# Handing part of a mixer's tail from VectorE and ScalarE to GpSimd, with two engines' work in another order

## What is computed

```python
def second_block(x, c, ...):
    h = _rms(x, norm1_w) * (1 + sc1) + sh1
    u, q, k, v = jnp.split(h @ w_in, ...)
    y_ssm  = _s5(u, ...)                       # 512 wide, 32 groups of 64 complex states
    y_attn = _swa_sink(_rms(q), _rms(k), v, rel_bias, sinks)   # 8 query heads, 2 kv heads, window 128
    mixed = concat(_rms(y_ssm, out_norm_ssm), _rms(y_attn, out_norm_attn))
    x = x + g1 * (mixed @ w_out)
    x = x + g2 * _conv_ffn(_rms(x, norm2_w) * (1 + sc2) + sh2, ...)

def _s5(u, ...):
    s = associative_scan(a * s + b u)          # complex states: s_re, s_im
    z = gelu(s_re @ c_re - s_im @ c_im + d * u)
    return z * sigmoid(z @ w_glu + b_glu)
```

## Time and profile before

| | us |
|---|---|
| median of 3 runs | 1794.73 |
| lowest to highest | 1794.62 to 1794.98 |
| the profiled execution | 1793.39 |
| its span, first to last instruction | 1791.9 |

### The profile page before, as it was taken

The page is one execution under the profiler, slowest core; times in us unless marked ns, Lnnn a source line. Parts: engine busy times, 40 slices in busy tenths (PEclk is TensorE's granted clock), DMA queues, the critical chain, the costliest instruction groups (busy, mean ns, idle before and its releaser), DMA issues. The chain is left out here.

```text
span 1791.9 us, 23429 instructions
## 1 busy us (share of the span) xinstructions
PE 1763.9 (98%) x8822; PEld 1437.1 (80%) x8822; DVE 1069.7 (60%) x1507; ACT 729.3 (41%) x1001; POOL 186.1 (10%) x239
## 2 busy tenths in 40 slices
PE   9999999999999999999999999999999999999998
PEld 6888888888887777788877888887986788888887
DVE  7666546655655676656888743436595655566433
ACT  4222222333435877423333222225465355555322
POOL 4222001210000000005211110210000300000000
PEclk9999999999999999999999999999999999999999
DMA  7777423343222121224554552325122222222232
GB/s 246 238 221 221 134 74 96 98 138 99 90 95 94 48 66 53 71 94 150 173 188 125 158 158 66 107 93 187 68 79 68 93 95 94 94 94 82 94 95 81
DMA packets 171694, 206.81 MB, mean 115 GB/s; under 512 B 18404, under 2 KB 150114, under 8 KB 171106
## 3 DMA queue, kind: packets, MB, share of 16 engines
q1 hardware_dynamic: 144994, 161.97, 27.9%
q0 software_dynamic: 12640, 38.55, 6.7%
q10 hardware_dynamic: 13984, 5.27, 1.1%
HBM read 190.29 MB, written 17.56 MB: 116 GB/s over the span
## 5 line engine op out<-in xcount | busy, mean ns | idle before, releaser
L692 ACT CAST w_hi<-w_raw 128x2048 fp32r<-128x2048 f32 x158 | 301.8, 1911 | 722.4 <-PE bank L2004 360.9
L1188 DVE TENSOR_TENSOR w_lo<-w_raw,w_hi 128x2048 fp32r<-128x2048 f32 x158 | 367.3, 2325 | 358.4 <-ACT w_hi L692 357.7
L2004 PE MATMUL bank<-h_hi,w_hi 128*128 128x512 f32 x1056 | 412.3, 390 | 3.5 <-DVE w_lo L1188 2.2
L2004 PE MATMUL bank<-h_hi,w_lo 128*128 128x512 f32 x1056 | 411.1, 389 | 0.0
L2004 PE MATMUL bank<-h_lo,w_hi 128*128 128x512 f32 x1056 | 325.4, 389 | 1.6 <-DVE h_lo L1231 1.6
L2004 PEld LDWEIGHTS bank<-h_hi,w_hi 128*128 128x128 f32 x1056 | 198.2, 188 | 49.5 <-issue 3.4
L2004 PEld LDWEIGHTS bank<-h_lo,w_hi 128*128 128x128 f32 x1056 | 198.2, 188 | 43.3 <-DVE h_lo L1231 2.0
L2004 PEld LDWEIGHTS bank<-h_hi,w_lo 128*128 128x128 f32 x1056 | 198.3, 188 | 41.0
L1961 PE MATMUL bank<-hid_hi,w_hi 128*128 128x512 f32 x528 | 205.6, 389 | 0.0
L1961 PE MATMUL bank<-hid_hi,w_lo 128*128 128x512 f32 x528 | 205.4, 389 | 0.0
L1961 PE MATMUL bank<-hid_lo,w_hi 128*128 128x512 f32 x528 | 205.4, 389 | 0.0
(11 more groups left out here) (442 smaller groups left out, 2464.8 us busy)
## 6 DMA issues: line engine op xcount, KB each, us to landing
w_raw<-in_w_in SPq DMA_DIRECT2D x29, 1024.0 KB, 5.0
mod_raw<-in_w_mod POOLq DMA_DIRECT2D x96, 256.0 KB, 4.1
w_raw<-in_ffn_w_gate SPq DMA_DIRECT2D x22, 1024.0 KB, 5.2
w_raw<-in_ffn_w_up SPq DMA_DIRECT2D x22, 1024.0 KB, 5.2
w_raw<-in_w_up SPq DMA_DIRECT2D x22, 1024.0 KB, 4.9
w_raw<-in_ffn_w_down SPq DMA_DIRECT2D x16, 768.0 KB, 4.6
w_raw<-in_ffn_w_down SPq DMA_DIRECT2D x16, 640.0 KB, 4.0
w_raw<-in_w_out SPq DMA_DIRECT2D x8, 1024.0 KB, 5.0
```

The costliest lines, as they stand in the source:

```text
L692: act.copy(w_hi[i % 2][:], w_raw[i % 2][:]).then_inc(S("w_hi_done"), 1)
L1188: dve.tensor_tensor(w_lo[s][:], w_raw[s][:], w_hi[s][:].bitcast(F32), ALU.subtract).then_inc(S("w_split"), 1)
L2004: mm = pe.matmul(bank[:], w[:, k, at], h[:, k, :], start=k == first and part == 0 and i == 0, stop=k == last and part == 1)
```

## The change

- POOL computes the second part (imaginary) of the states in both halves: two products with `rotc` into `tmp[:, 4:6]` and one sum of 504 columns. DVE keeps the first part, and waits ahead of the second half's products until both parts of the first half are made, since POOL reads the scans' results.
- POOL computes the low parts of two panels, `PART["glu"][0]` between the two halves of the states, and the next one after the squares of `yat`.
- POOL squares `yat` for query blocks 0 to 2 and adds the four tiles, so that one tile of 384 columns is left to TensorE's sum; ACT squares the last block alone, in one instruction. POOL squares the first three tiles of `ys` and adds them; ACT squares the fourth. TensorE sums five products (384 and 4 x 128 columns) for `pa` and two for `ps`, instead of four and four of 512.
- DVE takes the last unit's two copies to `pT` and the last two copies to `yat` (`sw_last`), between the first two and the last two tiles of `z_lo`.
- ACT runs `sw_exp(7)` ahead of `chunk_out(3)`; TensorE runs `within_chunks(3)` after `turn_back(1)` and `sw_turn(6)` ahead of `turn_back(3)`.

```diff
@@ pool
+            def split(n):
+                pool.wait_ge(S("w_hi_done"), n + 1)
+                pool.wait_ge(S("w_split"), n)
+                pool.tensor_tensor(w_lo[n % 2][:], w_raw[n % 2][:], w_hi[n % 2][:].bitcast(F32), ALU.subtract).then_inc(S("w_split"), 1)
+            def second_part(half):
+                own = slice(NS // 2 * half, NS // 2 * half + NS // 2)
+                parts = [tmp[:, 4 + i, :].rearrange("p (s c) -> p s c", c=NC) for i in range(2)]
+                pool.wait_ge(S("scanned"), NS * (half + 1))
+                for i in range(2):
+                    done(pool.tensor_tensor(parts[i], scan_t[:, 2 * i + 1], rotc[:, 1 - i, own], ALU.mult))
+                pool.tensor_tensor(state[:, 1, own, 1:NC], parts[0][:, :, 0:NC - 1], parts[1][:, :, 0:NC - 1], ALU.add).then_inc(S("scan_out"), 1)
+            second_part(0)
+            split(PART["glu"][0])
+            second_part(1)
+            pool.wait_ge(S("sw_s"), 2 * len(SW_UNITS))
+            for b in (0, 2):
+                at = slice(b * P, min(b + 2, 3) * P)
+                pool.wait_ge(S("sw_out"), 2 * min(b + 2, 3))
+                done(pool.tensor_tensor(yat_sq[:, :, at], yat[:, :, at], yat[:, :, at], ALU.mult))
+                done(pool.tensor_tensor(yat_sq[:, 0:2, at], yat_sq[:, 0:2, at], yat_sq[:, 2:4, at], ALU.add))
+                ins = pool.tensor_tensor(yat_sq[:, 0, at], yat_sq[:, 0, at], yat_sq[:, 1, at], ALU.add)
...
+            ins.then_inc(S("yat_squared"), 1)
+            split(PART["glu"][0] + 1)
+            for t in range(3):
+                pool.wait_ge(S("glu_out"), t + 1)
+                done(pool.tensor_tensor(ys_sq[:, t, :], ys[:, t, :], ys[:, t, :], ALU.mult))
+                if t:
+                    ins = pool.tensor_tensor(ys_sq[:, 0, :], ys_sq[:, 0, :], ys_sq[:, t, :], ALU.add)
...
+            ins.then_inc(S("ys_squared"), 1)
             norm("p2", "mix2")
@@ act
             chunk_out(2)
+            sw_exp(7)
             chunk_out(3)
-            sw_exp(7)
             sw_turned(6)
             s5_gelu((2,))
-            sw_turned(7)
             s5_gelu((3,))
-            sw_out(6)
-            sw_out(7)
             act.wait_ge(S("sw_out"), len(SW_UNITS))
-            for k in range(4):
-                act.activation(yat_sq[:, k, :], yat[:, k, :], ACT.Square).then_inc(S("yat_squared"), 1)
+            act.activation(yat_sq[:, :, 3 * P:], yat[:, :, 3 * P:], ACT.Square).then_inc(S("yat_squared"), 1)
...
-            for k in range(4):
-                act.wait_ge(S("glu_out"), k + 1)
-                act.activation(ys_sq[:, k, :], ys[:, k, :], ACT.Square).then_inc(S("ys_squared"), 1)
+            act.wait_ge(S("glu_out"), 4)
+            act.activation(ys_sq[:, 3, :], ys[:, 3, :], ACT.Square).then_inc(S("ys_squared"), 1)
@@ dve, chunks
+                if half:
+                    dve.wait_ge(S("scan_out"), 2)
...
-                for part, (first, second, op) in enumerate(((cosine, sine, ALU.subtract), (sine, cosine, ALU.add))):
-                    done(dve.tensor_tensor(t[0], t[1], first, ALU.mult))
-                    done(dve.tensor_tensor(t[2], t[3], second, ALU.mult))
-                    ins = dve.tensor_tensor(state[:, part, own, 1:NC], t[0][:, :, 0:NC - 1], t[2][:, :, 0:NC - 1], op)
...
+                done(dve.tensor_tensor(t[0], t[1], cosine, ALU.mult))
+                done(dve.tensor_tensor(t[2], t[3], sine, ALU.mult))
+                dve.tensor_tensor(state[:, 0, own, 1:NC], t[0][:, :, 0:NC - 1], t[2][:, :, 0:NC - 1], ALU.subtract).then_inc(S("scan_out"), 1)
@@ dve
+            def sw_last():
+                dve.wait_ge(S("sw_t_out"), SW_BEFORE[7])
+                dve.wait_ge(S("sw_pv"), 6)
+                for kb in SW_BLOCKS[7]:
+                    dve.wait_ge(S("sw_t"), SW_BEFORE[7] + kb + 1)
+                    dve.tensor_copy(pT[:, 1, kb, :], B[2 + kb][:]).then_inc(S("sw_t_out"), 1)
+                for u in (6, 7):
+                    b, n = SW_UNITS[u]
+                    dve.wait_ge(S("sw_pv"), u + 1)
+                    dve.tensor_copy(yat[:, 2 * n:2 * n + 2, b * P:(b + 1) * P], B[7][:, 0:2 * P].rearrange("p (j q) -> p j q", j=2)).then_inc(S("sw_out"), 1)
...
             sw_scale(6)
-            split(PART["glu"][0])
             sw_scale(7)
-            z_split(range(4))
-            split(PART["glu"][0] + 1)
+            z_split((0, 1))
+            sw_last()
+            z_split((2, 3))
@@ pe, norm
+                if name in ("pa", "ps"):
+                    bank = sum_bank(name)
+                    if name == "pa":
+                        pe.wait_ge(S("yat_squared"), 2)
+                        pe.matmul(bank[:, 0:3 * P], ones[:], yat_sq[:, 0, 0:3 * P], start=True, stop=True)
+                        mm = products(bank[:, 3 * P:], [(ones[:], yat_sq[:, k, 3 * P:]) for k in range(4)])
+                    else:
+                        pe.wait_ge(S("ys_squared"), 2)
+                        mm = products(bank[:], [(ones[:], ys_sq[:, t, :]) for t in (0, 3)])
+                    mm.then_inc(S("norm_summed"), 4)
+                    return
@@ pe
             within_chunks(2)
-            within_chunks(3)
             turn_back(0)
             sw_scores(6)
             sw_scores(7)
             sw_values(4)
             turn_back(1)
+            within_chunks(3)
             sw_values(5)
             from_states(2)
             from_states(3)
             turn_back(2)
+            sw_turn(6)
             turn_back(3)
-            sw_turn(6)
             sw_turn(7)
```

More of the change, by code:

```diff
@@ L673, in _ @@
             pool.dma_start(bias[:], bass.AP(band_dram, P - 1, [[BAND - 1, P], [P * BAND, NQ], [1, 2 * P]])).then_inc(S("bias_landed"), 16)
+            def split(n):
[19 more added lines that the diff above has]
+                ins = pool.tensor_tensor(yat_sq[:, 0, at], yat_sq[:, 0, at], yat_sq[:, 1, at], ALU.add)
+                if b == 0:
+                    done(ins)
+            ins.then_inc(S("yat_squared"), 1)
[5 more added lines that the diff above has]
+                    ins = pool.tensor_tensor(ys_sq[:, 0, :], ys_sq[:, 0, :], ys_sq[:, t, :], ALU.add)
+                    if t == 1:
+                        done(ins)
+            ins.then_inc(S("ys_squared"), 1)
             norm("p2", "mix2")
@@ L1796, in chunks @@
                 dve.wait_ge(S("scanned"), NS * (half + 1))
-                for part, (first, second, op) in enumerate(((cosine, sine, ALU.subtract), (sine, cosine, ALU.add))):
-                    done(dve.tensor_tensor(t[0], t[1], first, ALU.mult))
-                    done(dve.tensor_tensor(t[2], t[3], second, ALU.mult))
-                    ins = dve.tensor_tensor(state[:, part, own, 1:NC], t[0][:, :, 0:NC - 1], t[2][:, :, 0:NC - 1], op)
-                    ins.then_inc(S("scan_out"), 1)
-                    dve.wait_ge(S("scan_out"), 2 * half + part + 1)
+                done(dve.tensor_tensor(t[0], t[1], cosine, ALU.mult))
+                done(dve.tensor_tensor(t[2], t[3], sine, ALU.mult))
+                dve.tensor_tensor(state[:, 0, own, 1:NC], t[0][:, :, 0:NC - 1], t[2][:, :, 0:NC - 1], ALU.subtract).then_inc(S("scan_out"), 1)
             n = PART["q2"][0]
@@ L1973, in norm @@
                         square = tmp[:, d % 6, :]
[L1974 to L1979, removed]
                     else:
```

## The result

| | before | after |
|---|---|---|
| median, us | 1794.69 (9 runs, 1791.55 to 1796.57) | 1799.72 (9 runs, 1799.3 to 1805.05) |
| span of the profiled execution, us | 1791.9 | 1798.3 |
| VectorE busy, us | 1069.7 | 1080.0 |
| POOL busy, us | 186.1 | 217.9 |
| TensorE busy, us | 1763.9 | 1763.0 |

The changed kernel is slower: ratio 1.0034, 95% interval 1.0026 to 1.0043, so 4.7 to 7.7 us. The forecast was 1802.7 us in a range of 1793.5 to 1806.0. VectorE gave work away and is busy 10.3 us longer: the first sign that it stood still inside its instructions.

What follows compares the result with a forecast made beforehand. TensorE, busy 98% of the span, was taken as the bound. 9.2 - 1.93 + 1.9 - 1.72 + 0.1 = +7.5 us, with +0.5 for the clock +8.0, gave 1802.7 us; range 1793.5 to 1806.0.

Steps and rivals of the forecast that it cites:

- the clock: TensorE's turns, values and `glu(0)` after idling: between -1.6 us and +2 us, taken as +0.5 us.
- second rival: Tail: collisions spare the two probability multiplications, 1794.3 us; or long POOL instructions admit VectorE four times, 1799.4 us; chance 0.19.
- deciding step: Tail: VectorE and POOL, both reading SBUF, wait for each other's whole instruction; price its remainder less 0.14 us.
- first rival: Tail: VectorE runs free beside POOL, `glu(0)` 2.0 us earlier, sums give 3.65: -5.6, so 1789.1 us; chance 0.19.
- Step 1: States' first half: VectorE's and POOL's operations alternate, waits of 0.97 us each; the handed-over 2.1 us bring nothing.
- Steps 2 and 5: POOL's low parts delay unit 4's and 6's multiplications 4.6 and 4.5 us; `chunks(1)` 5.4 late, `sw_turn(6)` 10.5 late.
- Step 3: States' second half: operations alternate again; `sw_max(6)` starts at 1337.4 us, not 1332.1.
- Step 4: Squares of `yat` delay small operations of two maxima by 0.97 twice, 0.42, 0.58 us; exponentials at 1342.0, not 1336.0.
- Step 6: Before `glu(0)`: ScalarE's spared copies and VectorE's 2.28 us gone between units 6 and 7 return 1.3 us; `glu(0)` 9.2 late.
- Step 7: Norms: sums `pa` -1.93 us, waits beside POOL's squares of `ys` +1.9, sums `ps` -1.72, next panel's low part +0.1.

Runs made afterwards that it cites:

- e1: The changed kernel with both panels' low parts back on VectorE, at their places in the kernel before: 1796.75 us median, ratio to the kernel before 1.0004.
- e2: The changed kernel with each of POOL's low parts cut into four instructions of 512 columns: 1798.07 us.
- e3: The changed kernel with each of POOL's low parts replaced by two zero fills of the same tile, which read nothing: 1791.8 us.
- e7: The changed kernel with the states' second part back on VectorE, without the wait on it; POOL keeps low parts and squares: 1800.36 us.
- e4: The changed kernel with ten idle products in TensorE's wait ahead of `sw_turn(6)`: 1799.61 us.
- e10: The changed kernel with the last unit's `pT` copies and last two `yat` copies back on ScalarE, VectorE computing four z low parts together: 1799.54 us.
- e8: The changed kernel with the squares of `ys` back on ScalarE and four sums for the norm `ps`: 1801.69 us.
- e6: The kernel before with six idle products between `sw_values(6)` and `sw_values(7)`, nothing else: 1792.55 us.
- e5: The kernel before with VectorE adding squares in pairs, ScalarE squaring `ys` in gaps, and six idle products ahead of `sw_values(7)`: 1789.22 us median, ratio 0.997.

## Why the prediction was right

The sign, the mechanism and the range held; that the sum came out so near is in part luck, as said under the clock. The time alone would not have told: the second rival's variant, in which a long POOL instruction lets VectorE in four times, stood at 1799.4, nearer to the measured 1799.7 than the forecast's 1802.7. It is the timeline, with 5.28 and 5.21 us beside a POOL low part, that decides. Set against the measured stretch (us into it, after less before):

| step | forecast | measured |
|---|---|---|
| `chunks(1)` starts later by | 5.4 | 4.7 |
| `sw_max(6)` | 5.3 | 4.4 |
| exponentials of unit 6 | 6.0 | 4.9 |
| `sw_turn(6)` | 10.5 | 9.0 |
| `glu(0)` | 9.2 | 10.0 |
| end of the stretch | 8.0 | 7.4 |

**The deciding step**, that one waits for the whole of the other, is shown, not only argued: without POOL's long reads `sw_turn(6)` comes 8.02 us earlier and the loss falls by 5.96 (e1), with the same work in pieces it is 4.44 and 2.56 (e2), and with POOL writing only, the multiplications are undisturbed (e3). The Trainium skill's rule (SBUF — State Buffer, Who interferes with whom), that the pair is held for the whole instruction, agrees with 5.28 us beside 4.50 us. The price was right too: what is left of POOL's instruction less 0.14 is 1322.11 - 1317.91 - 0.14 = 4.06, and 5.28 - 1.22 = 4.06 was measured. The **second rival** falls: the multiplications with the spread operand wait like any other, and a long instruction lets nobody in. The **first rival** falls with it: VectorE is not free beside POOL.

**Step 1.** The waits of 0.97 came out as 0.96 and 0.94, and 1.06 on the sum of four columns; handing the states' second part over brought nothing, as said (e7). **Steps 2 and 5.** The mechanism was right, a size was off: a low part on POOL takes 4.50 us, not 4.9. The figure of the Trainium skill's GPSIMD Engine Reference (section Performance versus the Vector engine), 4.50, agrees with the trace and was the better one. Two low parts make 0.8 of the 1.5 us by which `sw_turn(6)` came earlier than forecast. The rest is smaller: POOL reached its first low part 5.12 us into the stretch, not 5.39, and led the multiplication by 0.30 us, not 0.15. **Step 3** follows. **Step 4** was too high: of the four waits of small operations, forecast at 0.97 twice, 0.42 and 0.58, the trace has 0.95, 0.34, 0.14 and 0.08: 1.5 us where the forecast had 2.94.

**Step 6.** From `sw_turn(6)` to `glu(0)` it took 8.94 us before and 10.01 after; at full clock (e4) 7.67, so 1.27 are given back, as the 1.3 of the forecast. But I put down a part of it to ScalarE's spared copies, and e10 refutes that: with them back the stretch is no longer. VectorE's low part between units 6 and 7, the other part of the step, is not the cause either as far as e1 shows: with it back the same passage takes 1353.25 - 1342.94 = 10.31 us, 0.30 more than after, and 0.24 of this is `sw_turn(7)` at the low clock (1.90 against 1.66). So the size of step 6 was right and its cause stays open; TensorE's new order, which the forecast put at 0.1 together with ScalarE's, was not tried alone.

**Step 7.** The sums gave 1.89 and 1.72, forecast 1.93 and 1.72. From the start of `glu(0)` to the end of the stretch took 42.95 us before and 40.29 after, 2.66 less; with 1.54 from the faster `glu(0)` and 3.61 from the sums, the norm beside POOL's squares cost 2.5, of which 0.9 is the clock's, so 1.6 where the forecast had 2.0.

**The clock** was the weak term. I gave it +0.5, a value between a `glu(0)` at full clock (-1.6) and slow turns and values besides a slow `glu(0)` (+2). What came was a part of each. It cost 2.3 in the turns ahead (e4), returned 1.54 in `glu(0)`, and took 0.9 more behind the norm, where the forecast had nothing (e8): **+1.7** in all. So the part without the clock, forecast at 7.5, came to 7.37 - 1.7 = 5.7, 1.5 of the difference being there at `sw_turn(6)`. The two errors, 1.8 too much and 1.2 too little, are of opposite sign, and that is why 8.0 against 7.4 looks better than the working was.

A slip in the chances: "slower" was put at 0.60 + 0.06 = 0.66 and leaves out the 0.02 for slower still, "faster" stands at 0.20 where the first rival has 0.19. It changes nothing here.

Of the 7.37 us, 5.0 (by the medians) to 6.1 (by the ratio) passed into the time. The forecast added the whole shift to the median; the two profiled executions, 6.4 apart in their spans, had tails that began 0.97 apart, which no change in the tail explains.

## What to carry to other kernels

Before work is handed to an idle GpSimd, look at what VectorE does at the same time. Here, where both read SBUF and VectorE with two tensors, the handed-over rotation products gained nothing (e7), and a low part that costs VectorE 2.28 us itself held it for 4.0 us from GpSimd, on whatever stood at that place. Work that is given to it should be short pieces (e2), or lie beside VectorE work with an operand in a bank (the additions of the bias, L1871, took 1.27 us beside POOL and 1.29 before). Idle time of an engine is no room by itself; the slots of the engines that are already in the chain (VectorE's pair sums, ScalarE between two gates) gave what GpSimd could not.

## What the runs showed of the hardware

- An instruction of four columns waits as long as one of 512: 1.21 us instead of 0.15 (L1884), beside POOL's sum.
- Not only instructions with two SBUF tensors wait: VectorE's `tensor_scalar` of four columns, with one, lasted 1.12 us instead of 0.17 (L1878). The maxima over 1024 columns, also with one, did not (L1875, 1.22 us beside POOL's 1.89).
- The hold works at 4.5 us as at 1.3: the waiting product ends 0.55 us behind POOL's instruction, 4.90 beside 4.77 (e7).
- A fill of 2048 columns by POOL takes 1.80 us, and VectorE's multiplications run beside it undisturbed (e3); a two-tensor operation of 2048 columns takes 4.50, of 512 columns 1.29, a square (the same tensor twice) of 512 columns 1.04, of 1024 1.89.
- An idle stretch of TensorE was paid for behind it: 2.3 us in the turns of after, 1.5 in `glu(0)` of before. Not each one was: after stood still 1.76 us ahead of `glu(0)` and ran it at clock 1.00. Idle products moved this cost where they started with the clock down (e6) and saved it where they started in time (e4, e5).
